# Moving the silu of the conditioning rows behind the fourth unit of the first rise

## The reference, cut to what matters

```
s_lat = silu(c)          # 1024 values, for the latents
s_ctx = silu(c_ctx)      # 1024 values, for the context
for li in range(2):
    m_lat = split(s_lat @ w_ada[li] + b_ada[li], 6)
    m_ctx = split(s_ctx @ w_ada[li] + b_ada[li], 6)
    ...
    h  = rms_norm(x,   g_ffn[li]) * (1 + m_lat[4]) + m_lat[3]
    x  = x + m_lat[5] * conv_ffn(h, ...)
    hc = rms_norm(ctx, g_ffn[li]) * (1 + m_ctx[4]) + m_ctx[3]     # layer 0 only
    ctx = ctx + m_ctx[5] * conv_ffn(hc, ...)

conv_ffn(h): z = h @ w_up (1024 -> 5632); z = conv of width 3 over tokens + bias
             g, v = split(z, 2);  return (silu(g) * v) @ w_down
```

## Time and profile before

| | |
|---|---|
| three executions | 2035.87, 2046.46, 2050.81 us |
| the profiled execution | 2047.51 us, its span 2045.7 us |
| PE busy | 1969.7 us, 96% of the span |
| PEld busy | 1667.0 us, 81% |
| DVE busy | 1388.8 us, 68% |
| ACT busy | 844.3 us, 41% |
| POOL busy | 143.4 us, 7% |
| mean granted clock of TensorE | 0.987 of full speed |

### The profile page before, as it was taken

The page is one execution under the profiler, slowest core; times in us unless marked ns, Lnnn a source line. Parts: engine busy times, 40 slices in busy tenths (PEclk is TensorE's granted clock), DMA queues, the critical chain, the costliest instruction groups (busy, mean ns, idle before and its releaser), DMA issues.

```text
span 2045.7 us, 31490 instructions
## 1 busy us (share of the span) xinstructions
PE 1969.7 (96%) x12385; PEld 1667.0 (81%) x12385; DVE 1388.8 (68%) x2227; ACT 844.3 (41%) x1332; POOL 143.4 (7%) x240
## 2 busy tenths in 40 slices
PE   8999999999999899979999999999999899999999
PEld 6777776577788778768888889997788786999999
DVE  6764424656448584568887768787468657688997
ACT  5621113744346543321111124444346445566754
POOL 0001000000030010000000000000040100000000
PEclk9989999999999999989999999999999999999999
DMA  5223135522362457658898844554362767855564
GB/s 195 72 62 103 56 103 195 197 87 82 132 178 77 186 131 176 168 186 282 220 270 216 264 117 133 176 165 135 133 186 67 206 183 229 223 186 184 180 202 160
DMA packets 92255, 332.62 MB, mean 163 GB/s; under 512 B 9872, under 2 KB 10896, under 8 KB 85088
## 3 DMA queue, kind: packets, MB, share of 16 engines
q1 hardware_dynamic: 73952, 199.78, 30.3%
q0 software_dynamic: 16656, 128.22, 23.3%
q10 hardware_dynamic: 1520, 2.85, 0.4%
HBM read 315.60 MB, written 99.09 MB: 203 GB/s over the span
## 4 chain that ended last, share of the span: by engine, by line
PE 78%; DMA 9%; DVE 8%; ACT 4%; issue 2%; ACTq 0%; POOL 0%; DVEq 0%
PE psum L237 21%; PE psum L239 20%; PE psum L238 20%; DMA fall_sums<-in_w_fall 7%; PE psum L896 3%; PE psum L857 2%; PE psum L884 2%; DMA fall_sums<-fall_sums 1%; PE psum L670 1%; PE psum L2221 1%; PE psum L1597 1%; PE psum L2093 1%; PE psum L245 1%; PE psum L1623 1%; PE psum L1615 1%
## 5 line engine op out<-in xcount | busy, mean ns | idle before, releaser
L237 PE MATMUL psum<-h_high,unit_high 128*128 128x512 f32 (+2 forms) x1548 | 539.5, 349 | 24.8 <-DVE unit_low L567 13.7
L239 PE MATMUL psum<-h_high,unit_low 128*128 128x512 f32 (+2 forms) x1548 | 526.0, 340 | 0.0
L238 PE MATMUL psum<-h_low,unit_high 128*128 128x512 f32 (+2 forms) x1548 | 525.4, 339 | 0.0
L237 PEld LDWEIGHTS psum<-h_high,unit_high 128*128 128x128 f32 x1548 | 294.0, 190 | 62.4 <-DVE unit_low L567 13.9
L239 PEld LDWEIGHTS psum<-h_high,unit_low 128*128 128x128 f32 x1548 | 293.4, 190 | 30.4
L238 PEld LDWEIGHTS psum<-h_low,unit_high 128*128 128x128 f32 x1548 | 294.3, 190 | 28.8 <-issue 2.4
L559 ACT CAST unit_high<-ring 128x1024 fp32r<-128x1024 f32 x111 | 116.1, 1046 | 248.1 <-PE psum L239 248.1
L567 DVE TENSOR_TENSOR unit_low<-ring,unit_high 128x1024 fp32r<-128x1024 f32 x111 | 135.4, 1220 | 61.8 <-ACT unit_high L559 61.8
L969 ACT ACTIVATE probs<-psum,neg_max 128x768 f32<-128x768 f32 (+4 forms) x136 | 98.6, 728 | 127.8 <-DVE neg_max L928 115.6
L928 DVE TENSOR_REDUCE neg_max<-psum 128x1 f32<-128x768 f32 (+4 forms) x136 | 97.3, 739 | 22.9 <-PE psum L857 21.8
L2878 DVE TENSOR_SCALAR conv_out<-psum,parameters 128x512 f32<-128x512 f32 x88 | 55.5, 672 | 78.4 <-PE psum L239 63.8
(11 more groups left out here) (512 smaller groups left out, 4096.9 us busy)
## 6 DMA issues: line engine op xcount, KB each, us to landing
ring<-in_w_units SPq DMA_DIRECT2D x237, 512.0 KB, 4.3
ring<-fall_sums SPq DMA_DIRECT2D x40, 512.0 KB, 3.7
fall_sums<-in_w_fall POOLq DMA_DIRECT2D x24, 768.0 KB, 7.0
block_sums<-in_w_blocks POOLq DMA_DIRECT2D x24, 768.0 KB, 9.0
ring<-block_sums SPq DMA_DIRECT2D x36, 512.0 KB, 3.6
ring<-in_w_fall SPq DMA_DIRECT2D x30, 512.0 KB, 3.7
ring<-in_w_blocks SPq DMA_DIRECT2D x27, 512.0 KB, 4.3
stacked_heads<-head_parts POOLq DMA_DIRECT2D x48, 192.0 KB, 4.9
```

Source lines behind the costliest of these rows:

```text
L237: pe.matmul(out, lh, rh, start=first, stop=False, skip_group_check=True)
L238: pe.matmul(out, lh, rl, start=False, stop=False, skip_group_check=True)
L239: return pe.matmul(out, ll, rh, start=False, stop=last, skip_group_check=True)
```

## The change

Three things are done. ScalarE's silu of the rows, with its wait for their load, is taken from ahead of the first unit and put behind the silu of the gate tile of unit 3 (j = 3 of turn 0), so ahead of the CAST of unit 5. VectorE's wait for that silu is put ahead of turn 1 instead of turn 0. GpSimd's wait names the count that the silu will reach, since the silu is now written further down in the program; GpSimd's own order stays as it was.

```diff
         if c_rows is not None:
-            @K.block.scalar
-            def _(act):
-                act.wait_ge(rows_in.sem, rows_in.n)
-                rows_ready.up(act.activation(rows_up[:, 0:2], rows_up[:, 0:2], ACT.Silu))
-
             @K.block.gpsimd
             def _(pool):
-                pool.wait_ge(rows_ready.sem, rows_ready.n)
+                pool.wait_ge(rows_ready.sem, rows_ready.n + 1)
                 rows_out.up(pool.dma_start(K.silu_rows, rows_up[:, 0:2]), 16)
...
                     split_high(K, act, i, j + 1)
                 activate(i, j)
+                if isinstance(i, int) and (i, j) == (0, 3):
+                    act.wait_ge(rows_in.sem, rows_in.n)
+                    rows_ready.up(act.activation(rows_up[:, 0:2], rows_up[:, 0:2], ACT.Silu))
...
-                dve.wait_ge(rows_ready.sem, rows_ready.n)
                 for a in (0, 1):
+                    if a:
+                        dve.wait_ge(rows_ready.sem, rows_ready.n)
                     for j in range(RING):
                         unit(a, j)
```

## The result

| | executions | median us | ratio to before, 95% interval |
|---|---|---|---|
| changed kernel, first series | 20 against 20 | 2040.16 against 2047.75 | 0.9959 [0.9943, 0.9976] |
| again (a1) | 12 against 30 | 2037.48 against 2050.22 | 0.9946 [0.9922, 0.9969] |
| again (f3) | 8 against 31 | 2036.47 against 2051.14 | 0.9914 [0.9879, 0.9949] |

The change makes the kernel faster, by about 8 us in the first series. The forecast was 2031 us within 2024 to 2038, 16 us under the profiled execution; the median fell outside the range. Weighted by their intervals the three ratios give 0.9949, that is 10.4 us, with an interval of 7.8 to 12.9 us; the three lie somewhat wider apart than their intervals alone would make likely.

The account below looks back on a forecast made before the run. TensorE's stall before unit 2 was held bound by a chain of transfers whose product it doesn't need yet. 13.82 + 2.11 - 0 = 15.93 us off 2047.51 gives 2031.6; forecast 2031 us, whole range 2024 to 2038.

Parts of the forecast that it names:

- the table load: ScalarE: would stand behind unit 2's CAST, under VectorE's convolution of unit 0; price 0, 1.3 us kept for the range.
- unit 3's subtraction: VectorE: would end at 876.77, 0.50 us before TensorE wants unit 3; the tightest place of the new schedule.
- the silu ran in its gap: ScalarE ahead of unit 5's CAST: the 1.91 us silu fits in 3.89 us of idle time; price 0.
- GpSimd's store: GpSimd's queue: the rows' store would be off it at 884.6, before the first block sum due at 886.05; price 0.
- Of the 13.82 us nothing is left by this sum: TensorE before unit 2: the 13.82 us delay vanishes, unit 2 starting at 868.94, when TensorE is free.
- I take both losses back: 13.82 + 2.11: TensorE at units 2 and 3: the 13.82 us delay and 2.11 us of half clock both go; unit 3 starts 15.93 us earlier.
- the executions closer together than 15 us: Sign in the profile after: executions spread by less than 15 us, as the chain no longer sets the time.
- the stall is as long as the 24 chained transfers make it: Before unit 2: the reason given for a gain over 1%; the 2050.81 run would have gained 19.3 us; chance 0.14.
- More than 1%: Rival, whole kernel: under 2026 us, if compared executions have a longer stall or the chain is slower; chance 0.14.
- Only the stall's main part goes: Rival, unit 2: VectorE misses its 0.50 us or the table load precedes the CAST; 2033 to 2036 us; chance 0.12.
- No change: Rival, unit 2: something hidden behind the silu, such as unit 2's weights, still holds TensorE; 2046 us; chance 0.03.
- Slower: Rival, unit 5: weight loads delay the rows' load, so TensorE waits; slower than before past a 35.5 us load; chance 0.02.

Follow-up runs that it names:

- e1: Kernel before, with the rows' load issued on ScalarE's queue behind the norm's rstd instead of behind GpSimd's chain of transfers; ratio to before 0.9926.
- e2: Kernel before with only VectorE's wait for the rows moved to turn 1, ScalarE's silu left at its head; ratio to before 0.9984.
- d1: Kernel before with 40 more matmuls on TensorE behind the norm's statistics, making TensorE late; ratio to before 1.0117.
- d2: Changed kernel with 40 more matmuls on TensorE behind the norm's statistics, making TensorE late; ratio to before 1.0108.
- c2: Changed kernel with the rows' load issued twice, one after the other, making the rows late; ratio to before 0.9944.
- f4: Kernel before run again without edits, for another profile; ratio to before 0.9998.
- g1: One execution of the kernel before, no edits, for another profile; 2043.36 us.
- g3: One execution of the kernel before, no edits, for another profile; 2049.64 us.
- f1: Changed kernel with ScalarE's silu of the rows two units earlier, behind the gate silu of unit 1; ratio to before 0.9950.
- b1: Kernel before run again without edits, for a second profile of its wait; ratio to before 0.9997.
- c1: Kernel before with the rows' load issued twice, one after the other, making the rows late; ratio to before 1.0033.
- f2: Changed kernel with the rows' load also issued on ScalarE's queue, as in e1; ratio to before 0.9932.
- g2: One execution of the changed kernel, no further edits, for another profile; 2041.58 us.
- g4: One execution of the changed kernel, no further edits, for another profile; 2033.53 us.

## Why the prediction was wrong

**The mechanism was right, step by step.** The wait went, the table load moved where it cost nothing, unit 3's subtraction came in time, the silu ran in its gap, and GpSimd's store was off the queue before the first block sum. Unit 2 took 10.44 us, part of it at half the clock, before and 8.22 after. e1, e2, d1 and d2 show cause and place.

**The step that failed is the first term of the sum,** "Of the 13.82 us nothing is left by this sum", together with "I take both losses back: 13.82 + 2.11". 13.82 was read from one execution, and a difference of two long ways of 172 us each, which vary by 5 and 11 us, is no constant. The profiled execution had one of the shortest ways of TensorE among the sixteen (172.3, where the mean is 175.1), with the clock granted almost wholly, and a chain of 173.3, a little over the mean. The mean wait by the formula is 10.1 us (standard error 1.1). With the 1.9 us by which unit 2 outlasts unit 3 in the seven profiles that have the wait, the gain is 12.0, give or take 2.3, against a measured 10.4 (7.8 to 12.9). What is left is within the error of both; late rows as in c2 would be one way to lose it. This mean takes the chains of both orders as one kind. The seven profiles with the wait alone give 12.6 + 1.9 = 14.5 us (standard error 1.1), 4 us over the measured gain, and if they are the fairer sample, some of the gain is lost at a place that these runs don't show.

A slip that changes no price: the 172.8 us from the first issue to the 24th hold 23 steps of 7.5 us and not 24 of 7.2, and the rows' load goes out 0.52 us behind the 24th issue, without waiting for its landing.

**The second failure is the base.** I took 2031.6 from the profiled execution and said that "the executions closer together than 15 us" would show the chain gone. They spread by 20.8 us in the first series, against 25.7 before. Most of the spread goes with TensorE's clock: over the 20 executions the correlation of time and granted clock is -0.89, from 2030.68 us at 0.994 to 2049.59 at 0.980. The profiled execution of before lay in the middle by its time (2047.51 us, the median of 20 is 2047.75), but only because a good clock and a long wait evened out: it had 0.987 where the mean of 30 later ones was 0.9846, an estimated 3.3 us by the slope of time on clock in those 30. Taking its wait away left its good clock in the forecast. So of the 8.6 us between 2031.6 and the measured 2040.16 some 3.9 are the wait and its half clock (15.93 against 12.0) and some 3.3 the clock, both estimates. Half clock behind the first transfer costs nothing in the kernel before, as the wait shrinks by it, and up to 5.5 us in the changed kernel (177.8 against 172.3). The rival "the stall is as long as the 24 chained transfers make it" saw one of the two moving ends; what it said of the run of 2050.81 has no trace behind it.

**The rivals.** "More than 1%" did not come: the first series lies under 0.6%. "Only the stall's main part goes" did not come either: VectorE and the table load were in time, and 2040 us lies above its 2033 to 2036. "No change" is out, for the three intervals stay below 1. "Slower" stayed far, though c2 shows its beginning; a rows' load beside weight loads took 8.7 to 9.9 us in the profiles of the changed kernel and 13.4 in c2 (the first of its two), against 8.3 to 8.7 in the kernel before; but in d1, where SP issued no load beside it, it took 10.1. By the rule of equal turns in the Trainium skill (DMA: Bandwidth & Descriptors, Queues, rings and completion order) such a load is slowed by SP's. The means point that way, d1 and e1 (10.1 each) blur it, and the 16.9 us estimated from the rule would have been too much.

## What to carry to other kernels

A wait at a point where two chains meet is a difference, and one profile gives one draw of it: before it is priced, find the start that both chains share, write both ways down, and ask what makes each vary. What slows the side that isn't critical is free until the wait is gone, and is paid in full after. Where work needs data that come behind a queue of transfers, either the data leave that queue or the work goes behind what doesn't need them; the two can't be told apart here.

## What the runs showed that I had not expected

**A second length of a unit.** The rise's units take either 8.21 or 8.32 to 8.33 us, all 40 of an execution alike (but four in c2, around its waits), at a granted clock of 1.00. Matmuls of 256 columns then follow each other every 113.3 or 117.8 ns. It is not the kernel: 8.21 in f4, g1 and g3 (before), d1, e2, f1, a1 and the first profile after; 8.32 or 8.33 in the first of before, b1, c1, e1, c2, d2, f2, f3, g2 and g4. The busy times of one stretch show it as a count of matmuls, first for f4 (the kernel before) and then f3 (the changed one):

```profile
1000.00:1050.00 50.00, 50.00 (x293) 43.98 (x292) 42.81 (x68) 8.84 (x9) 5.29 (x7) 1.00 0.94 243
```

```profile
1000.00:1050.00 50.00, 50.00 (x290) 44.01 (x289) 42.30 (x65) 8.85 (x9) 4.76 (x6) 1.00 0.90 221
```

Over 40 units this is 4 to 5 us, and it explains the rest of what the first pair of profiles differ by, 18.7 us: 16.0 from the first transfer to unit 3 and 4 to 5 in the rise, less 1.4 by which that transfer came later. What sets it stayed open.
